# Transposes of nine pre-norm tile passes: TensorE against the DMA crossbar

## The chip, the cores and the metric

The kernel runs on the eight cores of one Trainium2 chip. Every core runs the same program on its own share: half of one stream (2,048 frames in four tiles of 512) and two of the sixteen running streams (32 rows). Nothing is exchanged between cores. The metric is the time of the slowest core, in microseconds of device time. A core has a matrix engine (TensorE, PE), a vector engine (VectorE, DVE), a scalar engine (ScalarE, ACT), a general engine (GpSimd, POOL) and a sync engine (SyncE, SP). Each works through its own list of instructions in order and waits on semaphores; SP and POOL issue the DMAs.

## The reference

One layer has three sub-layers, each of which reads its input through a norm ("pre-norm") and adds a normed result to it:

```
def rmsnorm(x, g):
    y = x32 * lax.rsqrt(jnp.mean(jnp.square(x32), axis=-1, keepdims=True) + EPS)
    return (y * g).astype(x.dtype)

# sub-layer 1: pooling and a gated convolution of width 3 on xn @ w_in, group norms
xn = rmsnorm(x, g_mix_pre)
...
x = x + rmsnorm(merged @ w_out, g_mix_post)
# sub-layer 2: attention into 256 memory tokens, 4 heads of 256
x = x + rmsnorm(cross_attn(rmsnorm(x, g_x_pre), mem_k, mem_v, w_q, w_co), g_x_post)
# sub-layer 3: MLP 1024 -> 4096 -> 1024
hid = jnp.square(jax.nn.relu(rmsnorm(x, g_ff_pre) @ w_up))
x = x + rmsnorm(hid @ w_down, g_ff_post)
```

The pre-norm has two factors: one per row (the reciprocal root of the mean square) and one per column (g).

## The kernel before

The stream's rows lie on the 128 partitions when they are loaded (X, 128 rows x 1024 columns, fp32, eight buffers). A matmul needs the 1024 columns on the partitions. So each sub-layer begins, for each of the four tiles, with a **tile pass** (`pre_tile`, line 800): for each of four row tiles of 128 it calls `pre_sub` (line 759). That squares X on ScalarE with a sum (the output of the square, which nobody reads, goes into the buffer xs), makes the row factor of it in two small ScalarE instructions (Ln and Exp), scales X by it on VectorE into xs (bf16), transposes the eight 128x128 blocks of xs on TensorE into one PSUM bank, and brings the bank into xT on VectorE, multiplied by the column factors (gcs). There are two xs buffers and two xT buffers; xT holds one tile, 128 partitions x 8 blocks x 512 rows, bf16. Three sub-layers of four tiles are twelve tile passes; the memory tokens and the 32 rows of the running streams call `pre_sub` by themselves.

The consumers of xT are, per tile, the mixer's projections (`win`, in `pool_group` and `conv_group`), the query projections (`wq`, `qproj`, 64 matmuls) and the up-projection (`up_chunk`, 256 matmuls, weights up in three buffers of 1 MB, each of which POOL refills when TensorE has released it). A tile of attention is: query projections into qT, four heads (scores, the exponential pT on ScalarE, its sum and the value products on TensorE, the reciprocal rd in two ScalarE instructions, the product mg on VectorE), the output projection `wco`, and `post`, which adds to X. The MLP has a down-projection of 256 matmuls (`wdn`) after each up-projection. The order of tiles in attention is 2, 3, 0, 1; the X of tiles 0 and 1 was stored to x1 and is loaded again there.

The program is first written down as a list of operations with what they read and write. A planner (`Prog.schedule`, line 245) then gives each engine its order: at each moment it takes, of the operations that are ready by its own costs, the one written down first (`prio`), if PSUM has banks for it. A DMA is planned with 2.6 us and its bytes at 345 GB/s on SP (lines 242 and 243), 3.4 us for 256 KB. The emitted lists are fixed: on the chip an engine stands at an instruction whose semaphores are late, and all that follows in its list stands with it. Nearly all instructions are recorded by helpers, so one line of the profile stands for many: L633 matmuls, L638 transposes, L662 activations, L669 VectorE's products of two tensors, L677 its products with a column, L682 its three-operand form, L690 and L692 copies, L701 DMAs.

Of the kernel before, what the change touches and what calls it, by code (L numbers as in the profile page):

```python
# [9 lines left out]
AF = mybir.ActivationFunctionType  # L10
ALU = mybir.AluOpType
# [6 lines left out]
TN = 512  # L18
NSUB = 4
# [493 lines left out]
def build_program():  # L513
# [161 lines left out]
    def ts(out, in0, s1, op0, per=0.5):  # L675
        rdl = [in0] + ([] if isinstance(s1, float) else [s1])
        P.add([("dve", lambda e, L: e.tensor_scalar(out=L(out), in0=L(in0), scalar1=s1, scalar2=None, op0=op0),  # L677
                c_dve(ncols(out), per))], reads=rdl, writes=[out])
# [34 lines left out]
    def r3(ap, n):  # L713
        return ap.rearrange("p (c t) -> p c t", c=n)
# [6 lines left out]
    def stat(r, n=1):  # L721
        a = stn[0]
        stn[0] += n
        assert stn[0] <= 512
        return st[0:r, a:a + n]
# [24 lines left out]
    def rstd(ss, r):  # L750
        a = stat(r)
        b = stat(r)
        act(a, ss, AF.Ln, scale=1.0 / D, bias=epsb[0:r, 0:1])
        act(b, a, AF.Exp, scale=-0.5)
        return b
# [3 lines left out]
    def pre_sub(X, r, gc, dst):  # L759

        ss = stat(r)
        xs = xsr[xs_n[0] % 2][0:r, :]
        xs_n[0] += 1
        act(xs, X, AF.Square, accum=ss)
        rs = rstd(ss, r)
        ts(xs, X, rs, ALU.mult)
        ps = PS(1, reserve=1)
        for c in range(8):
            tr(ps.v(0, 128, c * 128, c * 128 + r, BF16), xs[:, c * 128:(c + 1) * 128], idb[0:r, 0:r])
        src = ps.v(0, 128, 0, 1024, BF16, lambda a: r3(a, 8)[:, :, 0:r])  # L770
        gb = gcs[:, gc * 8:(gc + 1) * 8].unsqueeze(2).to_broadcast([128, 8, r])
        tt(dst, src, gb, ALU.mult)
# [17 lines left out]
    def load_tile(t, src, lead=LEAD):  # L790
# [6 lines left out]
            ops.append(load(b[:, :], src[row:row + 128, :], 524288, lead=lead, rd=(src is not xp)))  # L797
        return ops

    def pre_tile(t, gc, buf):  # L800
        for i in range(NSUB):
            dst = r3(buf[:, :], 8)[:, :, i * 128:(i + 1) * 128]
            pre_sub(Xof[(t, i)][:, :], 128, gc, dst)
# [393 lines left out]
    def load_down(a, b, after=None):  # L1197
        for k in range(a, b):
            wload(dparts[k][:, :], wdn_d, 8 * k, 8 * k + 8, after)
# [57 lines left out]
    for t in range(2, NT):  # L1257
        for g in range(4):
            step(pool_group(t, g))
            if t == 2:  # L1260
                kv_block(g)
                if g < 2:
                    kv_loads(g + 2)
        for cc in range(4):
            step(conv_group(t, cc))
            if cc == 1 and t + 1 < NT:
                pre_tile(t + 1, 0, xT[(t + 1) % 2])
            elif cc == 1:
                pre_tile(2, 1, xT[0])
        step(None)  # L1270
        if t == NT - 1:
            state_out()
            wload(wco[:, :], wco_d, 0, 16)
        else:
            wload(wq[:, :], wq_d, 0, 16)
        mix_out(t)
# [3 lines left out]
    for p, t in enumerate((2, 3, 0, 1)):  # L1280
        for j in range(8):
            qproj(p, j)
        if p == 1:
            smp_q()
        if p == 3:
            load_down(2, 4)
        fins = []
        for hh in range(4):
            step(attn_head(p, hh))
            if hh == 1 and p < 3:  # L1290
                pre_tile((3, 0, 1)[p], 1, xT[(p + 1) % 2])
            elif hh == 1:
                pre_sub(Xe[0:NS, :], NS, 2, r3(xTe[:, :], 8)[:, :, 0:NS])
                pre_tile(0, 2, xT[0])
        step(None)
        if p == 1:
            smp_attn()
            load_down(0, 2)
        out_tile(t, lambda kc, p=p: mg[p % 2][:, kc * TN:(kc + 1) * TN], 8, wc, gslot["g_x_post"],
                 x2 if t >= 2 else None)  # L1300
        if p < 2:
            load_tile(p, x1)
        if p == 0:
            for k in range(3):
                load_up(0, k)
        if p == 1:
            out_smp(lambda kc: mgs[:, kc * NS:(kc + 1) * NS], 8, wc, gslot["g_x_post"])
    load_gp("g_ff_post")
    ups = None
    for t in range(NT):  # L1310
        for k in range(8):
            for jj in range(4):
                up_chunk(t, k * 4 + jj)
            if t == 0:
                if k % 4 == 0:
                    ups = PS(1)
                up_smp(k, ups)
            n = k + 3
            if n < 8:
                op = load_up(t, n)  # L1320
                if t == 0 and n == 7:
                    load_down(4, 8, op)
            elif t + 1 < NT:
                load_up(t + 1, n - 8)
        if t + 1 < NT:
            pre_tile(t + 1, 2, xT[(t + 1) % 2])
        out_tile(t, hid, 32, wd, gslot["g_ff_post"], yp)
        if t == 0:
            out_smp(lambda kc: hids[:, kc * NS:(kc + 1) * NS], 32, wd, gslot["g_ff_post"])
            dma("sp", ysm[:, :], Xe[0:NS, :], NS * 4096, wr=False)  # L1330
        if t + 2 < NT:
            load_tile(t + 2, x2)
# [100 lines left out]
```

How the kernel before makes its waits and increments, by code:

```python
        def run(e, eng):  # L458
            seen = {}
            for op in seqs[e]:
                waits = {}
                for p in plan[op]:
                    k, v = (p.sem, p.semval) if p.is_dma else (p.eng, p.sigval)
                    if seen.get(k, 0) >= v:
                        continue
                    if waits.get(k, 0) < v:
                        waits[k] = v
                for k, v in waits.items():
                    eng.wait_ge(dsem[k] if isinstance(k, tuple) else esem[k], v)
                    seen[k] = v
                ins = op.fn(eng, lambda x: x.resolve(psum) if isinstance(x, PV) else x)
                if op.is_dma:
                    ins.then_inc(dsem[op.sem], 16)
                elif op.needs_signal:
                    ins.then_inc(esem[e], 1)
            if e == "sp":
                for k, last in dma_last.items():
                    if seen.get(k, 0) < last.semval:
                        eng.wait_ge(dsem[k], last.semval)
```

The softmax here doesn't subtract the row's maximum and nothing guards it: scores larger than these inputs give would overflow.

## Time and profile before

| | us |
|---|---|
| median of 3 runs (915.09, 916.25, 1033.09) | 916.25 |
| the profiled execution | 913.83 |
| its span, slowest core | 912.3 |
| the eight cores' spans | 901.6 to 912.3 |
| TensorE, busy time in the span | 858.4 |
| VectorE | 396.1 |
| ScalarE | 383.8 |
| GpSimd | 113.4 |

The highest of the three runs fell into a disturbed state of the chip and is left out of comparisons. Engine busy times count the instructions' own durations, overlaps taken out; since matmuls overlap one another (each is listed with some 0.38 us and begins 0.216 us after the one before), distances between starts tell what a matmul costs. In rows of the timeline, a number in brackets at the end is the time for which the engine was idle before, and what ended that. In rows of a stretch ("A:B") the numbers are its length, then the busy times of PE, PEld, DVE, ACT and POOL with their instruction counts, the granted TensorE clock (1.00 is the 2.4 GHz level), the mean busy share of the DMA engines, and GB/s. In rows of DMA issues: how often, KB each, median us from issue to landing.

### The profile page before, as it was taken

How to read it: one execution, taken by the hardware profiler on the slowest of the kernel's cores; microseconds unless marked ns; L12 is line 12 of the kernel's file. 1: busy time of each engine (PE TensorE's matmuls, PEld its weight loads, DVE VectorE, ACT ScalarE, POOL GpSimd, SP SyncE). 2: the span in 40 equal slices, each digit the busy share in tenths (PEclk: the TensorE clock that was granted, in tenths of full speed). 3: DMA queues.
4: the chain of work that ended last, by engine and by line, in shares of the span. 5: the costliest groups of instructions: out<-in, count | busy, mean ns of one | idle time of the engine just before them, and what ended most of it. 6: DMA issues, size and time to landing. Idle time of an engine off the chain costs nothing.

```text
span 912.3 us, 13810 instructions; the slowest of 8 cores (901.6 to 912.3 us)
## 1 busy us (share of the span) xinstructions
PE 858.4 (94%) x4708; PEld 407.1 (45%) x4708; DVE 396.1 (43%) x545; ACT 383.8 (42%) x808; POOL 113.4 (12%) x164
## 2 busy tenths in 40 slices
PE   1679998899999999999999999999999999999996
PEld 1334445444445454445445444444444444444442
DVE  4547659566875556546523131323222412222212
ACT  4456647556776565656434031332223410133101
POOL 4363100611520000000012000110001100010000
PEclk9989999999999999999999999999999999999999
DMA  9994054952459629006499962698218981088011
GB/s 236 146 156 64 1 174 149 199 87 44 63 82 174 192 50 241 13 1 93 73 147 145 155 175 70 95 152 129 73 66 145 142 129 47 32 122 124 1 46 47
DMA packets 69801, 97.61 MB, mean 107 GB/s; under 512 B 2618, under 2 KB 60218, under 8 KB 69732
## 3 DMA queue, kind: packets, MB, share of 16 engines
q0 software_dynamic: 58384, 58.85, 46.3%
q1 hardware_dynamic: 11348, 37.87, 12.1%
q8 instruction: 39, 0.64, 0.3%
q14 instruction: 30, 0.25, 0.1%
HBM read 137.50 MB, written 18.07 MB: 171 GB/s over the span
## 4 chain that ended last, share of the span: by engine, by line
PE 85%; DMA 8%; DVE 2%; ACT 2%; issue 1%; SPq 0%; POOL 0%; DVEq 0%; ACTq 0%; POOLq 0%
PE ps L633 83%; PE ps L638 2%; DMA wkv_108<-w_v 2%; DMA win<-w_in 1%; DMA up_129<-w_up 1%; DMA X_63<-xp 1%; DMA x<-X_65 1%; DMA O_58<-mem 1%; DMA X_65<-x 1%; DVE O_58 L669 0%; DVE mg_83 L669 0%; ACT rf_106 L662 0%; SPq L701 0%; ACT sq_104 L662 0%; DVE xT_55 L669 0%
## 5 line engine op out<-in xcount | busy, mean ns | idle before, releaser
L669 DVE TENSOR_TENSOR O_57<-ps,gp 128x1024 f32<-128x1024 f32 (+1 forms) x26 | 31.7, 1221 | 120.0 <-PE ps L633 73.7
L662 ACT ACTIVATE O_57<-ps 128x1024 f32<-128x1024 f32 (+1 forms) x26 | 26.5, 1021 | 125.0 <-PE ps L633 123.6
L669 DVE TENSOR_TENSOR O_58<-ps,gp 128x1024 f32<-128x1024 f32 (+1 forms) x25 | 30.6, 1222 | 96.0 <-PE ps L633 61.9
L662 ACT ACTIVATE rt_128<-ps 128x512 bf16<-128x512 f32 x64 | 38.2, 597 | 72.5 <-PE ps L633 64.5
L662 ACT ACTIVATE rt_127<-ps 128x512 bf16<-128x512 f32 x64 | 38.2, 596 | 70.3 <-PE ps L633 70.3
L633 PE MATMUL ps<-xT_55,win 128*128 128x512 bf16 x256 | 62.8, 395 | 4.6 <-DVE xT_55 L669 2.5
L662 ACT ACTIVATE O_58<-ps 128x1024 f32<-128x1024 f32 (+1 forms) x25 | 25.6, 1023 | 96.0 <-PE ps L633 94.6
L633 PE MATMUL ps<-xT_56,win 128*128 128x512 bf16 x256 | 62.2, 394 | 0.4 <-DVE mg_84 L682 0.4
L633 PE MATMUL ps<-xT_56,up_129 128*128 128x512 bf16 x192 | 42.4, 379 | 0.5 <-DMA up_129<-w_up 0.4
L633 PE MATMUL ps<-xT_55,up_130 128*128 128x512 bf16 x192 | 42.4, 379 | 0.0
L633 PEld LDWEIGHTS ps<-xT_55,win 128*128 128x128 bf16 x256 | 25.1, 101 | 34.9 <-issue 9.3
L633 PEld LDWEIGHTS ps<-xT_56,win 128*128 128x128 bf16 x256 | 25.7, 101 | 32.5 <-issue 5.8
L669 DVE TENSOR_TENSOR xT_56<-ps,gcs 128x1024 bf16<-128x1024 bf16 x24 | 28.9, 1219 | 22.5 <-PE ps L638 22.2
L669 DVE TENSOR_TENSOR xT_55<-ps,gcs 128x1024 bf16<-128x1024 bf16 x24 | 28.9, 1218 | 16.2 <-PE ps L638 10.6
L633 PE MATMUL ps<-xT_56,up_131 128*128 128x512 bf16 x160 | 35.4, 379 | 0.0
L633 PE MATMUL ps<-xT_56,up_130 128*128 128x512 bf16 x160 | 35.3, 379 | 0.0
L633 PE MATMUL ps<-xT_55,up_129 128*128 128x512 bf16 x160 | 35.3, 379 | 0.0
L633 PE MATMUL ps<-xT_55,up_131 128*128 128x512 bf16 x160 | 35.3, 379 | 0.0
L633 PE MATMUL ps<-wdn_132,hid_123 128*128 128x512 bf16 x128 | 33.5, 379 | 0.0
L633 PE MATMUL ps<-wdn_135,hid_124 128*128 128x512 bf16 x128 | 33.2, 379 | 0.0
L633 PE MATMUL ps<-wdn_134,hid_124 128*128 128x512 bf16 x128 | 33.0, 379 | 0.0
L633 PE MATMUL ps<-wdn_133,hid_123 128*128 128x512 bf16 x128 | 33.0, 379 | 0.0
(356 smaller groups left out, 1521.4 us busy)
## 6 DMA issues: line engine op xcount, KB each, us to landing
up_129<-w_up POOLq DMA_DIRECT2D x11, 1024.0 KB, 11.4
up_130<-w_up POOLq DMA_DIRECT2D x11, 1024.0 KB, 12.3
up_131<-w_up POOLq DMA_DIRECT2D x10, 1024.0 KB, 10.8
win<-w_in POOLq DMA_DIRECT2D x4, 768.0 KB, 27.7
wout<-w_out POOLq DMA_DIRECT2D x1, 2048.0 KB, 46.2
wq<-w_q POOLq DMA_DIRECT2D x1, 2048.0 KB, 16.5
wco<-w_co POOLq DMA_DIRECT2D x1, 2048.0 KB, 16.3
X_61<-xp SPq DMA_DIRECT2D x2, 512.0 KB, 6.4
```

The costliest lines, as they stand in the source:

```text
L633: P.add([("pe", lambda e, L: e.matmul(L(out), lhsT=lhsT, rhs=rhs, start=start, stop=stop, skip_group_check=True), max(0.03, n * 0.000421 + ...
L638: P.add([("pe", lambda e, L: e.transpose(out=L(out), in_=in_, identity=idn), 0.065 if in_.dtype == BF16 else 0.25)], reads=[in_, idn], wri ...
L662: return e.activation(out=L(out), in_=L(in_), func=func, scale=scale, **kw)
L669: opts.append(("dve", lambda e, L: e.tensor_tensor(out=L(out), in0=L(in0), in1=L(in1), op=op), c_dve(n, per)))
```

## The change

`pre_tile_dma` takes the place of `pre_tile` in nine of the twelve passes: the mixer's tile 3, the four of attention and the four of the MLP. The mixer's first three passes, the memory tokens and the running streams keep `pre_sub`. In the new function xs is transposed by one DMA per row tile (`dma_start_transpose`, from SBUF into SBUF, 256 KB, on SP's queue), which writes straight into xT. The column factor is then applied in place, after all four row tiles have landed, by eight VectorE instructions of 128x512, one for each block of columns. The planner is told 0.06 us for the issue, 262,144 bytes, and a quarter of the usual cost per element for the eight products.

In attention the pass for the next tile is also written down earlier: ahead of the four heads, not after the second one. So it stands before all of them in `prio`.

```
+    def pre_tile_dma(t, gc, buf):
+        for i in range(NSUB):
+            X = Xof[(t, i)][:, :]
+            ss = stat(128)
+            xs = xsr[xs_n[0] % 2][:, :]
+            xs_n[0] += 1
+            act(xs, X, AF.Square, accum=ss)
+            rs = rstd(ss, 128)
+            ts(xs, X, rs, ALU.mult)
+            dst = r3(buf[:, :], 8)[:, :, i * 128:(i + 1) * 128]
+            P.add([("sp", lambda e, L, dst=dst, xs=xs: e.dma_start_transpose(out=dst, in_=xs), 0.06)],
+                  reads=[xs], writes=[dst], nbytes=262144)
+        for c in range(8):
+            v = buf[:, c * TN:(c + 1) * TN]
+            ts(v, v, gcs[:, gc * 8 + c:gc * 8 + c + 1], ALU.mult, per=0.25)
...
             if cc == 1 and t + 1 < NT:
-                pre_tile(t + 1, 0, xT[(t + 1) % 2])
+                pre_tile_dma(t + 1, 0, xT[(t + 1) % 2])
             elif cc == 1:
-                pre_tile(2, 1, xT[0])
+                pre_tile_dma(2, 1, xT[0])
...
+        if p < 3:
+            pre_tile_dma((3, 0, 1)[p], 1, xT[(p + 1) % 2])
+        else:
+            pre_sub(Xe[0:NS, :], NS, 2, r3(xTe[:, :], 8)[:, :, 0:NS])
+            pre_tile_dma(0, 2, xT[0])
         fins = []
         for hh in range(4):
             step(attn_head(p, hh))
-            if hh == 1 and p < 3:
-                pre_tile((3, 0, 1)[p], 1, xT[(p + 1) % 2])
-            elif hh == 1:
-                pre_sub(Xe[0:NS, :], NS, 2, r3(xTe[:, :], 8)[:, :, 0:NS])
-                pre_tile(0, 2, xT[0])
...
         if t + 1 < NT:
-            pre_tile(t + 1, 2, xT[(t + 1) % 2])
+            pre_tile_dma(t + 1, 2, xT[(t + 1) % 2])
```

The planner makes a new order of it. Three places, all in the third attention pass (p = 2), in which X_65 to X_68 are the four row tiles of the next pass. First ScalarE, before (a row with xs on the left is a Square, pT the exponential, rd the reciprocal, qT the eviction of a query projection):

```order
L662 ACTIVATE xs_59,st<-X_65 128x1024 [waits d_sp_13]
L690 ACTIVATE qT_112<-ps 128x512 [waits s_pe]
L662 ACTIVATE st<-st,epsb 128x1 [waits s_act]
L662 ACTIVATE st<-st 128x1 [waits s_act]
L662 ACTIVATE xs_60,st<-X_66 128x1024 [waits d_sp_15]
L662 ACTIVATE st<-st,epsb 128x1 [waits s_act]
L662 ACTIVATE st<-st 128x1 [waits s_act]
L690 ACTIVATE qT_112<-ps 128x512 [waits s_pe] x4
L662 ACTIVATE pT_116<-ps 128x1024 [waits s_pe]
L662 ACTIVATE pT_117<-ps 128x1024 [waits s_pe]
L662 ACTIVATE xs_59,st<-X_67 128x1024 [waits d_sp_17,s_dve,s_pe]
```

and now:

```order
L662 ACTIVATE xs_60,st<-X_66 128x1024 [waits d_sp_32,d_sp_26]
L690 ACTIVATE qT_112<-ps 128x512 [waits s_pe]
L662 ACTIVATE st<-st,epsb 128x1 [waits s_act]
L662 ACTIVATE st<-st 128x1 [waits s_act]
L690 ACTIVATE qT_112<-ps 128x512 [waits s_pe]
L662 ACTIVATE xs_59,st<-X_67 128x1024 [waits d_sp_33,s_dve,d_sp_35]
L690 ACTIVATE qT_112<-ps 128x512 [waits s_pe]
L662 ACTIVATE st<-st,epsb 128x1 [waits s_act]
L662 ACTIVATE pT_116<-ps 128x1024 [waits s_pe]
L662 ACTIVATE st<-st 128x1 [waits s_act]
L662 ACTIVATE pT_117<-ps 128x1024 [waits s_pe]
L662 ACTIVATE xs_60,st<-X_68 128x1024 [waits d_sp_34,s_dve,d_sp_36]
```

The third Square (X_67) stood behind both exponentials and waited for TensorE's transposes; it now stands ahead of them, among the query projections, and waits for d_sp_35, the first transposing DMA.

VectorE, before:

```order
L677 TENSOR_SCALAR xs_60<-X_66,st 128x1024 [waits d_sp_15,s_act]
L669 TENSOR_TENSOR xT_56<-ps,gcs 128x8x128 [waits s_pe] x2
L669 TENSOR_TENSOR mg_83<-ps,rd_118 128x512 [waits s_act]
L669 TENSOR_TENSOR mg_83<-ps,rd_118 128x512
L677 TENSOR_SCALAR xs_59<-X_67,st 128x1024 [waits d_sp_17,s_act]
L677 TENSOR_SCALAR xs_60<-X_68,st 128x1024 [waits d_sp_18,s_act]
L669 TENSOR_TENSOR xT_56<-ps,gcs 128x8x128 [waits s_pe] x2
L669 TENSOR_TENSOR mg_83<-ps,rd_119 128x512 [waits s_act]
```

and now:

```order
L677 TENSOR_SCALAR xs_59<-X_67,st 128x1024 [waits d_sp_33,s_act]
L669 TENSOR_TENSOR mg_83<-ps,rd_118 128x512 [waits s_pe,s_act]
L677 TENSOR_SCALAR xs_60<-X_68,st 128x1024 [waits d_sp_34,s_act]
L669 TENSOR_TENSOR mg_83<-ps,rd_118 128x512 [waits s_pe]
L669 TENSOR_TENSOR mg_83<-ps,rd_119 128x512 [waits s_pe,s_act]
L677 TENSOR_SCALAR xT_56<-xT_56,gcs 128x512 [waits d_sp_35,d_sp_36,d_sp_37,d_sp_38]
L677 TENSOR_SCALAR xT_56<-xT_56,gcs 128x512 x7
L669 TENSOR_TENSOR mg_83<-ps,rd_119 128x512 [waits s_pe]
```

The four evictions out of PSUM are gone; eight products wait for all four DMAs and have five of the eight mg products of the pass behind them.

TensorE there, now (idle spots aside, no transposes are left between the heads):

```order
L633 MATMUL ps<-pT_117,vS 128x512 [waits s_dve]
L633 MATMUL ps<-pT_117,vS 128x512
L633 MATMUL ps<-pT_116,ones 128x512 [waits s_act]
L633 MATMUL ps<-pT_116,ones 128x512
L633 MATMUL ps<-pT_116,vS 128x512 x2
L633 MATMUL ps<-pT_116,vS 128x512 [waits s_dve]
L633 MATMUL ps<-pT_116,vS 128x512
L633 MATMUL ps<-pT_117,ones 128x512 [waits s_act]
L633 MATMUL ps<-pT_117,ones 128x512
L633 MATMUL ps<-pT_117,vS 128x512 x4
L633 MATMUL ps<-wco,mg_83 128x512 [waits s_dve]
```

Between its waits for VectorE it has six, then eight matmuls.

## Rows read from the trace of the kernel before

**Rows 1.** The page: engines' busy time, and the chain that ended last, by line.

```profile
PE 858.4 (94%) x4708; PEld 407.1 (45%) x4708; DVE 396.1 (43%) x545; ACT 383.8 (42%) x808; POOL 113.4 (12%) x164
...
PE ps L633 83%; PE ps L638 2%; DMA wkv_108<-w_v 2%; DMA win<-w_in 1%; DMA up_129<-w_up 1%; DMA X_63<-xp 1%; DMA x<-X_65 1%; DMA O_58<-mem 1%; DMA X_65<-x 1%; DVE O_58 L669 0%; DVE mg_83 L669 0%; ACT rf_106 L662 0%; SPq L701 0%; ACT sq_104 L662 0%; DVE xT_55 L669 0%
```

**Rows 2.** Stretches of the span: loads and first tiles, mixer and attention, MLP.

```profile
0.00:190.00 190.00, 151.05 (x892) 75.27 (x892) 113.40 (x175) 106.25 (x233) 58.34 (x98) 0.96 0.68 138
190.00:426.00 236.00, 230.01 (x1399) 111.06 (x1398) 153.75 (x175) 149.68 (x314) 26.14 (x33) 1.00 0.52 98
426.00:903.90 477.90, 477.30 (x2422) 220.73 (x2420) 126.47 (x194) 126.25 (x258) 28.95 (x33) 1.00 0.59 100
```

**Rows 3.** Groups by form: count, busy us, mean ns, idle before.

```profile
L638 PE MATMUL ps<-idb,xs_60 128*128 128x128 bf16 x200 | 17.2, 226 | 7.3 <-DVE xs_60 L677 7.2
```

**Rows 4.** Timeline of TensorE at the end of an up-projection: start, us.

```profile
624.72 0.61 PE L638 MATMUL ps<-idb,xs_59 128*128 128x128 bf16 x8
625.17 0.81 PE L633 MATMUL ps<-wdn_132,hid_123 128*128 128x512 bf16 x3
```

**Rows 5.** Groups by form, VectorE: eviction into xT, scaling into xs, the square.

```profile
L669 DVE TENSOR_TENSOR xT_56<-ps,gcs 128x1024 bf16<-128x1024 bf16 x24 | 28.9, 1219 | 22.5 <-PE ps L638 22.2
L669 DVE TENSOR_TENSOR hid_123<-rt_127 128x512 bf16<-128x512 bf16 x16 | 6.8, 425 | 16.2 <-ACT rt_127 L662 16.2
L677 DVE TENSOR_SCALAR xs_60<-X_67,st 128x1024 bf16<-128x1024 f32 x4 | 3.0, 748 | 0.8 <-ACT st L662 0.8
```

**Rows 6.** DMA issues of 256 KB on SP.

```profile
mk<-O_58 SPq DMA_DIRECT2D x1, 256.0 KB, 4.0
mk<-O_57 SPq DMA_DIRECT2D x1, 256.0 KB, 8.5
mv<-O_58 SPq DMA_DIRECT2D x1, 256.0 KB, 3.2
mv<-O_57 SPq DMA_DIRECT2D x1, 256.0 KB, 2.3
```

**Rows 7.** The page: busy tenths of the DMA engines in 40 slices of 22.8 us.

```profile
DMA  9994054952459629006499962698218981088011
```

**Rows 8.** The MLP: issues and landing of up blocks, their use, TensorE's wait.

```profile
583.87 0.87 POOL L701 DMA_DIRECT2D up_129<-w_up  x1 [7.49 <-PE ps L633]
688.05 0.87 POOL L701 DMA_DIRECT2D up_130<-w_up  x1 [59.86 <-PE ps L633]
...
595.54 7.07 PE L633 MATMUL ps<-xT_56,up_129 128*128 128x512 bf16 x32
...
up_129<-w_up POOLq DMA_DIRECT2D x11, 1024.0 KB, 11.4
...
L633 PE MATMUL ps<-xT_56,up_129 128*128 128x512 bf16 x192 | 42.4, 379 | 0.5 <-DMA up_129<-w_up 0.4
```

**Rows 9.** Timeline of the third attention pass: two Squares, the last load of X.

```profile
359.01 1.06 ACT L662 ACTIVATE xs_59<-X_65 128x1024 bf16<-128x1024 f32 x1 [1.74 <-DMA X_65<-x]
...
370.85 1.06 ACT L662 ACTIVATE xs_59<-X_67 128x1024 bf16<-128x1024 f32 x1
...
362.82 0.32 SPq L701 DMA_DIRECT2D X_68<-x  x1
```

**Rows 10.** Timeline of VectorE there: the last two evictions, the products behind them.

```profile
376.63 2.36 DVE L669 TENSOR_TENSOR xT_56<-ps,gcs 128x1024 bf16<-128x1024 bf16 x2 [0.71 <-PE ps L638]
378.90 1.28 DVE L669 TENSOR_TENSOR mg_83<-ps,rd_119 128x512 bf16<-128x512 f32 x2
```

**Rows 11.** TensorE there, and the stretch of the heads.

```profile
374.15 1.02 PE L633 MATMUL ps<-qT_112,kT 128*128 128x512 bf16 x4 [0.88 <-DVE mg_83 L669]
375.70 0.38 PE L633 MATMUL ps<-qT_112,kT 128*128 128x512 bf16 x1 [0.53 <-ACT rd_119 L662]
...
368.00:382.00 14.00, 12.35 (x81) 6.13 (x78) 9.57 (x12) 11.91 (x23) 0.00 (x0) 1.00 0.00 0
```

## The prediction

> **What bounds the kernel now.** I read the engines' busy time first. TensorE is busy 94% of the span, no other engine over 45%, and the chain of work that ended last is 83% matmuls of one line and 2% transposes [rows 1]. Then I cut the span into stretches [rows 2]. Up to 190 us TensorE also waits for loads (151 of 190 us busy). From 190 to 426 us (last mixer tiles, attention) it is idle 6.0 us, from 426 us to its end (the MLP) 0.6 us. The granted clock there is 1.00. So in 714 us of the 912 us there is next to nothing to win but TensorE's own work, and work taken off it shows almost one for one, unless a new wait appears. All nine passes that the change touches put their transposes into this part; a few of the first pass fall just before it.
>
> **Step 1, what is removed.** There are 400 full-size bf16 transposes, 200 out of each of the two xs buffers [rows 3]: 12 tile passes and the two memory tiles, 50 row tiles of 8. Nine passes are 36 row tiles, 288 transposes. Their own duration, 226 ns, overlaps the next one's, so I take the distance between starts: a run of eight begins at 624.72, the next matmul at 625.17 [rows 4], 0.45 us per row tile. 36 × 0.45 = **16.2 us** of TensorE. With them go 36 evictions of 1.22 us on VectorE [rows 5], 4.9 us a pass, and a PSUM bank for each.
>
> **Step 2, what is added: 36 crossbar DMAs of 256 KB on SP's queue.** No row shows one. Call T the time from issue to landing. The nearest rows are the other 256 KB transfers that SP issues, both between SBUF and HBM: 2.3, 3.2, 4.0 and 8.5 us [rows 6]; the two longer ones belong to the eighth slice of the span, where the DMA engines are at 9 tenths, the two shorter to the ninth, at 5 [rows 7]. I take 3.5 us, among the three lower ones, because of the slices from 274 to 433 us, in which the attention passes lie, the DMA share is 9 in two, 6 in two and 2 or less in three; 2.3 and 8.5 are the bounds. Against this speaks the Trainium skill, "VectorE: DVE Perf Modes", the section on the three transpose paths, which gives 1309 ns for a 128x128 bf16 block through the crossbar and 390 ns on TensorE. Eight blocks one after another would make an estimate of T of 10.5 us, and the sum below would then come out slower than before. No run here shows either figure.
>
> Where T falls decides. In the three MLP passes the result is wanted a whole down-projection later (in one of them POOL stood 59.86 us for TensorE [rows 8]), so I cost them at nothing; cover gone, it is rival A. In the six others three engines wait in order. ScalarE's third Square writes the buffer that the first DMA still reads, and the order shows it in front of the exponentials. In the third attention pass the first and third Squares were 11.84 us apart (359.01 and 370.85) [rows 9], so T under some 8 us hides there; the new order moves them closer, which is free while TensorE does projections. VectorE waits longer: the eight column products wait for all four DMAs and stand ahead of the attention products (the mg rows), for which TensorE waits. The row that ends the last scaling now has two products (0.64 us each, 1.28 for two [rows 10]) before that wait, so VectorE stands T − 1.3 us.
>
> **Step 3, the column products.** A 128x512 product of bf16 in SBUF by a column has no row. The scaling of 1024 columns from fp32 takes 0.75 us, half of that 0.37; the bf16 square of two inputs 0.425 [rows 5]. I take 0.37, 3.0 us a pass. In the same place VectorE was idle 0.71 us and evicted for 2.36 [rows 10], 3.1 us. So a pass makes VectorE later by (T − 1.3) + 3.0 − 3.1 = T − 1.4, at T = 3.5 by 2.1 us, six times 12.6 us. That is the upper end, if TensorE pays all of it. The lower end is a gain: the Squares leave the crowded head phase, VectorE does less, and the 6.6 us of idle time in the two stretches could go. Of +12.6 and −6.6 I take the middle, **+3 us**: ScalarE was a cause of TensorE's waits in those passes (0.53 us for a reciprocal, 0.88 us for a product [rows 11]), which helps, and the wait for the DMA is new, which does not.
>
> SP's own queue: it issues the stores and loads of X as before, and issuing takes some 0.3 us each. In the third attention pass its four DMAs stand behind the last load of X, which was issued at 362.82 [rows 9], 3.8 us after the first Square began; a row tile takes nearly that long to be scaled, so it costs about a microsecond, and that lies before the wait above. POOL's loads are not passed by anything. The clock is at its 2.4 GHz level throughout (1.00), so there is nothing to gain or lose in it.
>
> **Sum.** 913.83 (the profiled execution, span 912.3 and 1.5 around it) − 16.2 + 3 = 900.6. The median of the three runs is 916.25 and the lowest 915.09, 2.4 and 1.3 above that execution; I add 1.9: **902.5 us**. Its own range is 892.9 (16.2 and 6.6 gained) to 912.1 (16.2 gained, 12.6 lost).
>
> **Rivals.**
> A, the weight stream. In the MLP a 1 MB block of up weights is issued when a buffer is released and lands in 11.4 us; one issued at 583.87 was used at 595.54, 11.7 us later [rows 8], so little is spare. Four transposes move as much as one block through the same 16 DMA engines. At 2.3 us each that is 9.2 us; if a third of it meets the loads (four of a tile's twelve block times), that is some 3 us a tile, 9 us in three: 911.5. For it: the DMA share there is near full [rows 7] and TensorE waited for such a load already [rows 8]. Against it: the new order has two of the three tiles loaded, and so transposed, mostly in the down-projection before, in which POOL issues nothing (up to 688 us in the row). Chance 0.12.
> B, slower: the crossbar DMA is long. If T is 8.5, VectorE is late by T − 1.4 = 7.1 us in each of six passes. TensorE has some 2 us of work there that needs no product of VectorE's (six and eight matmuls between its waits for VectorE in the new order, of 7.07/32 = 0.22 us each [rows 8], 3.0 in all, less the waits for ScalarE among them), so it pays 5.1, six times 30.6: 913.8 − 16.2 + 30.6 + 1.9 = 930. It decides from T = 6.1 on, where six times (T − 3.4) eats the 16.2 us. For it: the row of 8.5 us [rows 6], and that the crossbar's cost is in no row; against it: three of the four 256 KB rows are at or under 4 us. Chance 0.15. By the estimate from the page above, T = 10.5, it would be 942.
> C, TensorE's transposes only filled waits. In a head phase, from 368 to 382 us, ScalarE is busy nearly all the time, and TensorE, transposes included, still waited [rows 11]. If ScalarE sets the end there, four attention passes give back nothing: 4 × 4 × 0.45 = 7.2 us less gained, 909.7. Against it: TensorE waited only 6.0 us in 236 [rows 2], and the Squares leave that phase. Chance 0.16.
>
> **Numbers.** My forecast has 0.57. Within 2% of 916.25 means 897.9 to 934.6, about what a measurement of this kernel can tell from no change. Under 897.9 lies the lowest quarter of the forecast's range, 0.14 of the chance; I take 0.13, since A and C can come on top of it. Over 934.6 lies half of B, 0.08. The rest, 0.79, is within. The range 893 to 922 takes in the forecast's own, A and C, and A and C with some of the 12.6; it leaves out most of B and a little below, together under 0.2.
>
> **What would show it.** Step 1: the 128x128 bf16 transposes fall from 400 to 112, and TensorE's busy time by about 16 us. Step 2: the rows of xT from xs on SP land in 3 to 4 us; VectorE's waits for them total under 6 × 2.2 us. Step 3: the new products take 0.2 to 0.4 us each. TensorE's idle time after 190 us should be near 10 us: 25 or more there means B (VectorE waiting for xT's DMAs, TensorE for mg) or A (TensorE waiting for up loads); the same end with 7 us more idle time and no DMA named is C. The forecast is wrong if a DMA lands in over 6 us, or if the stretch before 190 us, which the new order also touches, moves by more than 5 us.

## The result, and the profile after

The changed kernel takes 977.06 us (median of 4 runs, 973.89 to 978.45) beside 916.01 us before: **ratio 1.0665, 95% interval 1.063 to 1.070**, slower by 61 us where 902.5 was forecast. Of the experiments below, replan and all9fix have no ratio, since in all or half of their runs part of the cores ran at a lower granted clock than the rest; their times and spans stand instead.

The profiled execution took 978.45 us, its slowest core (core 6) 976.9. The page's busy times and chain, against [rows 1]:

```profile
PE 865.5 (89%) x4420; PEld 395.5 (40%) x4420; DVE 373.3 (38%) x579; ACT 382.1 (39%) x811; POOL 113.9 (12%) x163
...
PE ps L633 73%; DMA xT_56<-xs_59 3%; DMA xT_55<-xs_59 3%; DMA xT_56<-xs_60 2%; DMA X_67<-xp 2%; DMA up_129<-w_up 1%; DMA win<-w_in 1%; DMA X_63<-xp 1%; PE ps L638 1%; DMA O_57<-mem 1%; SPq L811 1%; DVE xs_59 L677 1%; ACT st L662 1%; DVE xT_
```

The stretches, against [rows 2] (length, busy times of PE, PEld, DVE, ACT, POOL, granted clock, DMA share, GB/s):

```profile
0.00:190.00 190.00, 148.57 (x869) 73.44 (x870) 112.08 (x174) 105.98 (x235) 58.70 (x98) 0.96 0.71 142
190.00:426.00 236.00, 206.17 (x986) 89.47 (x985) 120.50 (x169) 127.78 (x269) 24.36 (x30) 0.90 0.58 108
426.00:976.90 550.90, 510.78 (x2568) 232.64 (x2566) 140.67 (x238) 148.31 (x308) 30.84 (x35) 0.97 0.60 99
```

TensorE was to lose 16.2 us of work; its busy time *rose* by 7.1 us (858.4 to 865.5), and its idle time from 53.9 to 111.4. So the account is: −16.2 for the transposes, +57.5 of idle time, and a remainder of +23.3, beside which stands a lower clock (0.90 and 0.97, where [rows 2] has 1.00): 64.6, the difference of the spans. Worked out from the granted clock during TensorE's busy time, the loss by the clock is 6.4 us before and 30.5 now, 24.1 more. Some 8.5 of it lie in three stretches of 15 us (from 281.7, 340.8 and 380.2 on), in which TensorE was busy throughout and the clock was 0.81; cores 2 and 3, with spans of 964.2 and 961.8 us, have no such stretch, and what brings it is not shown. One of the three:

```profile
340.80:355.80 15.00, 15.00 (x59) 6.20 (x57) 4.48 (x6) 9.34 (x21) 0.00 (x0) 0.81 0.77 203
```

The groups by form show that the change did what it says (against [rows 3, 5]; the products are new):

```profile
L669 DVE TENSOR_TENSOR xT_55<-ps,gcs 128x1024 bf16<-128x1024 bf16 x8 | 9.6, 1217 | 6.0 <-PE ps L633 5.1 <-PE ps L638 1.0
...
L677 DVE TENSOR_SCALAR xT_56<-xT_56,gcs 128x512 bf16<-128x512 bf16 x40 | 11.5, 352 | 24.8 <-DMA xT_56<-xs_59 22.1 <-DMA xT_56<-xs_60 2.7
...
L638 PE MATMUL ps<-idb,xs_60 128*128 128x128 bf16 x56 | 5.1, 244 | 6.7 <-DVE xs_60 L677 6.7
```

112 transposes are left of 400, 12 evictions of 48, and 72 products cost 0.35 us each. What is out of line is the transposing DMA (L811), by source line: issues on SP, who waited for it, and its time to landing.

```profile
L811 SPq DMA_TRANSPOSE xT_56<-xs_60 x10: 1233/1446/7582, 160.5 to 746.2; - x10
L811 SPq DMA_TRANSPOSE xT_56<-xs_59 x10: 1232/1254/10129, 170.1 to 758.2; - x10
...
  DVE xT_56 L677: 24.8, 3
  ACT xs_59 L662: 19.1, 3
  DVE xT_55 L677: 12.4, 3
  ACT xs_60 L662: 6.2, 2
...
DMA to landing us min/median/max: 3.0/3.1/19.1
```

The median is 3.1 us, the longest 19.1. One by one, 27 of the 36 land in 3.0 to 4.7 us, nine in 10.5 to 19.1. These nine have one thing in common, a load that POOL had issued:

| issued at | landed after, us | loads of POOL in flight then (issue to landing) |
|---|---|---|
| 160.5, 170.1 | 17.5, 16.4 | w_v (157.8 to 173.9, 165.2 to 185.6) |
| 242.0 | 13.8 | wco (239.0 to 257.8) |
| 287.1, 289.1 | 13.7, 19.1 | two of w_up (274.3 to 301.8), ckT, cv (281.4 to 308.9, 282.3 to 314.2) |
| 449.8 | 14.7 | two of w_down (445.6 to 465.3) |
| 499.4, 501.1 | 13.4, 18.6 | three of w_up (495.0 to 520.7) |
| 758.2 | 10.5 | three of w_up (748.1 to 774.1) |

A load that had only just been issued, or was nearly through, cost a DMA under 2 us. Counted in the trace, 1,428 to 2,747 packets of POOL's queue were moved between the issue and the landing of each of the nine; for 24 of the 27 others it was none, for three 8, 253 and 530.

The first attention pass, 284 to 324 us, shows what that cost. Its first two DMAs, from the DMA view of 286:292, and POOL's loads of that time:

```profile
xT_56<-xs_59 SPq DMA_TRANSPOSE x1, 13.7
xT_56<-xs_60 SPq DMA_TRANSPOSE x1, 19.1
```

```profile
281.44 0.88 POOL L701 DMA_DIRECT2D kTs<-ckT  x1 [5.38 <-PE ps L633]
282.31 0.89 POOL L701 DMA_DIRECT2D vSs<-cv  x1
```

ScalarE there; in brackets the idle time before and what ended it:

```profile
300.95 1.06 ACT L662 ACTIVATE xs_59<-X_67 128x1024 bf16<-128x1024 f32 x1 [6.54 <-DMA xT_56<-xs_59]
302.00 1.00 ACT L662 ACTIVATE pT_116<-ps 128x1024 bf16<-128x1024 f32 x1
...
308.34 1.06 ACT L662 ACTIVATE xs_60<-X_68 128x1024 bf16<-128x1024 f32 x1 [5.15 <-DMA xT_56<-xs_60]
...
309.78 1.00 ACT L662 ACTIVATE pT_117<-ps 128x1024 bf16<-128x1024 f32 x1
```

The third and fourth Square (X_67, X_68) write the xs buffers that these DMAs still read, and an exponential (pT) stands right behind each. VectorE, and then TensorE:

```profile
286.87 0.75 DVE L677 TENSOR_SCALAR xs_60<-X_66,st 128x1024 bf16<-128x1024 f32 x1
309.68 0.75 DVE L677 TENSOR_SCALAR xs_59<-X_67,st 128x1024 bf16<-128x1024 f32 x1 [22.07 <-ACT st L662]
...
316.21 2.19 DVE L677 TENSOR_SCALAR xT_56<-xT_56,gcs 128x512 bf16<-128x512 bf16 x8 [2.74 <-DMA xT_56<-xs_60]
318.32 1.28 DVE L669 TENSOR_TENSOR mg_83<-ps,rd_119 128x512 bf16<-128x512 f32 x2
```

```profile
303.15 1.01 PE L633 MATMUL ps<-pT_116,ones 128*128 128x512 bf16 x2 [6.08 <-ACT pT_116 L662]
...
310.93 1.01 PE L633 MATMUL ps<-pT_116,vS 128*128 128x512 bf16 x2 [4.77 <-ACT st L662]
...
321.95 3.49 PE L633 MATMUL ps<-wco,mg_83 128*128 128x512 bf16 x10 [2.21 <-DVE mg_83 L669]
```

VectorE stood 22.07 us for the row factor of the third row tile, then waited for the last DMA with mg behind the products; TensorE waited for the exponential (6.08), for the next one (4.77; it went on 0.15 us after that one's end) and for mg (2.21). It then ran slowly as well. The same stretch of the span, now and before:

```profile
284.00:324.00 40.00, 26.92 (x149) 11.19 (x148) 10.85 (x21) 16.13 (x31) 0.00 (x0) 0.76 0.94 146
```

```profile
284.00:324.00 40.00, 39.13 (x254) 19.03 (x252) 23.79 (x26) 23.87 (x51) 0.00 (x0) 1.00 0.78 173
```

Here, with 13.1 us of idle time in it, the clock is 0.76 on average over 40 us; before it was 1.00.

In the fourth attention pass the DMA issued at 449.8 held ScalarE's fourth Square for 11.04 us, with the reciprocals behind it, and so TensorE:

```profile
468.58 6.71 PE L633 MATMUL ps<-wco,mg_84 128*128 128x512 bf16 x20 [11.67 <-DVE mg_84 L669]
```

In the MLP, VectorE and TensorE at the end of the first up-projection:

```profile
503.68 0.43 DVE L669 TENSOR_TENSOR hid_124<-rt_128 128x512 bf16<-128x512 bf16 x1 [0.85 <-ACT rt_128 L662]
519.84 0.62 DVE L677 TENSOR_SCALAR xT_56<-xT_56,gcs 128x512 bf16<-128x512 bf16 x2 [15.74 <-DMA xT_56<-xs_59]
520.37 0.42 DVE L669 TENSOR_TENSOR hid_124<-rt_127 128x512 bf16<-128x512 bf16 x1
```

```profile
520.94 0.58 PE L633 MATMUL ps<-wdn_134,hid_124 128*128 128x512 bf16 x1 [12.62 <-DVE hid_124 L669]
```

The planner had put the second tile's pass into the up-projection; its products stand ahead of hid, which the down-projection reads.

Where the time goes stage by stage (us from the span's start, worked out as the median of the eight cores; a few matmuls that stand ahead of the long run of their stage are left out):

| first matmul of | before | after | stage up to it: longer by | long DMAs in it |
|---|---|---|---|---|
| query projections | 265.1 | 278.4 | 13.3 | 3 |
| wco, pass 1 | 292.2 | 320.6 | 15.1 | 2 |
| wco, pass 2 | 332.9 | 365.0 | 3.7 | 0 |
| wco, pass 3 | 377.1 | 414.4 | 5.2 | 0 |
| wco, pass 4 | 418.2 | 466.0 | 10.5 | 1 |
| wdn, tile 1 | 492.2 | 558.1 | 18.1 | 2 |
| wdn, tile 2 | 619.6 | 681.1 | −4.4 | 0 |
| wdn, tile 3 | 731.9 | 797.1 | 3.7 | 1 |
| wdn, tile 4 | 844.5 | 906.3 | −3.4 | 0 |
| (end of wdn) | 897.7 | 959.6 | 0.1 | 0 |

The five stages with a long DMA lost 61 us, the five without lost 1.

### The profile page after: what moved, and what is told of

Its sections match the earlier page's. It is cut to its first block, busy times and chain, and to the rows that moved or that the text cites. A ratio compares the mean times of both kernels' runs of the same rounds, so it can differ in the third digit from the quotient of the medians.

```text
span 976.9 us, 13473 instructions; the slowest of 8 cores (961.8 to 976.9 us)
## 1 busy us (share of the span) xinstructions
PE 865.5 (89%) x4420; PEld 395.5 (40%) x4420; DVE 373.3 (38%) x579; ACT 382.1 (39%) x811; POOL 113.9 (12%) x163
## 3 DMA queue, kind: packets, MB, share of 16 engines
q1 hardware_dynamic: 49364, 47.31, 18.1%
## 4 chain that ended last, share of the span: by engine, by line
PE 74%; DMA 14%; DVE 4%; ACT 3%; issue 3%; SPq 1%; POOL 0%; ACTq 0%; DVEq 0%; POOLq 0%
PE ps L633 73%; DMA xT_56<-xs_59 3%; DMA xT_55<-xs_59 3%; DMA xT_56<-xs_60 2%; DMA X_67<-xp 2%; DMA up_129<-w_up 1%; DMA win<-w_in 1%; DMA X_63<-xp 1%; PE ps L638 1%; DMA O_57<-mem 1%; SPq L811 1%; DVE xs_59 L677 1%; ACT st L662 1%; DVE xT_56 L677 0%; ACT xs_59 L662 0%
## 5 line engine op out<-in xcount | busy, mean ns | idle before, releaser
L633 PE MATMUL ps<-xT_55,up_130 128*128 128x512 bf16 x192 | 44.0, 387 | 4.2 <-ACT rt_128 L662 2.9
L633 PE MATMUL ps<-wdn_134,hid_124 128*128 128x512 bf16 x128 | 33.7, 381 | 12.6 <-DVE hid_124 L669 12.6
L633 PE MATMUL ps<-xT_56,up_129 128*128 128x512 bf16 x192 | 42.4, 379 | 1.9 <-DMA up_129<-w_up 1.9
L633 PE MATMUL ps<-wco,mg_84 128*128 128x512 bf16 x128 | 32.2, 418 | 12.8 <-DVE mg_84 L669 11.7
L633 PE MATMUL ps<-xT_55,up_129 128*128 128x512 bf16 x160 | 36.8, 390 | 0.0
L633 PE MATMUL ps<-xT_56,up_131 128*128 128x512 bf16 x160 | 35.4, 379 | 0.0
L633 PE MATMUL ps<-xT_55,up_131 128*128 128x512 bf16 x160 | 35.3, 379 | 0.0
L633 PE MATMUL ps<-xT_56,up_130 128*128 128x512 bf16 x160 | 35.3, 379 | 0.0
L633 PE MATMUL ps<-wco,mg_83 128*128 128x512 bf16 x128 | 29.9, 394 | 5.1 <-DVE mg_83 L669 5.1
L633 PE MATMUL ps<-wdn_132,hid_123 128*128 128x512 bf16 x128 | 33.5, 379 | 0.0
L633 PE MATMUL ps<-wdn_133,hid_123 128*128 128x512 bf16 x128 | 33.3, 379 | 0.0
L633 PE MATMUL ps<-wdn_135,hid_124 128*128 128x512 bf16 x128 | 33.2, 379 | 0.0
## 6 DMA issues: line engine op xcount, KB each, us to landing
up_129<-w_up POOLq DMA_DIRECT2D x11, 1024.0 KB, 11.6
up_130<-w_up POOLq DMA_DIRECT2D x11, 1024.0 KB, 13.2
wq<-w_q POOLq DMA_DIRECT2D x1, 2048.0 KB, 18.1
wco<-w_co POOLq DMA_DIRECT2D x1, 2048.0 KB, 18.8
```

The costliest lines, as they stand in the source:

```text
L633: P.add([("pe", lambda e, L: e.matmul(L(out), lhsT=lhsT, rhs=rhs, start=start, stop=stop, skip_group_check=True), max(0.03, n * 0.000421 + ...
```

## The experiments

**Theory**: a transposing DMA moves 256 KB as 1,024 packets of 256 B, and these take turns with the packets of a weight load on the same DMA engines; where the two meet it is long, and the in-order engines pass the wait on. **Rivals**: the crossbar itself is slow in company; the new order, the buffers or the wait as such cost, whatever the DMA takes. In the diffs, − is the changed kernel unless said otherwise. Ratios are to the kernel before on the same chip, with 95% intervals. Only copy256 has the changed kernel's order on TensorE, VectorE and ScalarE, instruction for instruction; after every other edit the planner made another order, so those times hold its effect too, and the landings of the DMAs are the firmer evidence.

**1. mlp3 and six: which passes.** mlp3 has `pre_tile_dma` in the MLP's three passes alone, with the order of before in attention; six has it in the other six alone (`pre_tile(t + 1, 2, ...)` in the MLP).

> Only the three passes of the MLP go by DMA; the other nine are as in the kernel before. Turn-taking theory (a transposing DMA is 1,024 packets of 256 B and each waits for the packets of a weight load that is in flight on the same DMA engines; without one it lands in 3.1 us): one or two of the twelve DMAs fall into an up load and take 10 us or more, and cover hides most of it: 916 - 5.4 (12 row tiles of 0.45 us) + 0 to 5 = 911 to 916. Rival A of the prediction (the DMAs delay the up loads): 919 or more, with TensorE waiting for up blocks by 9 us more than before.

> Only the mixer's tile 3 and the four passes of attention (and the first of the MLP, written there) go by DMA; the three MLP passes keep TensorE. Turn-taking theory: eight of the nine long DMAs of the changed kernel (13 to 19 us) lie here, so nearly the whole loss is here: 970 to 980. If the loss were spread evenly over the nine passes: 916 + 61 x 6/9 = 957.

Measured: mlp3 1.0027 (0.9994 to 1.0061), six 1.0526 (1.0500 to 1.0553). Most of the loss is in the six, but at 958.8 us less than the 970 to 980 expected and close to the 957 of an even spread. The expectation had miscounted: six of the nine long DMAs lie in these passes, not eight (and six has six, of 14.1 to 20.0 us). The two parts, 0.3 and 5.3%, make less than the 6.7% of all nine together. In mlp3 two of twelve DMAs were long (8.3 and 10.2 us); the second, a last row tile beside an up load, made VectorE wait with hid behind it, then ScalarE, and so TensorE:

```profile
704.46 3.57 PE L633 MATMUL ps<-xT,up 128*128 128x512 bf16 x8 [4.02 <-ACT rt L662]
```

With a clock of 0.50 (the 1.2 GHz level) in 703.7:710.3, that takes back the 5.4 us gained. Rival A's price did not show: of TensorE's waits over 0.5 us one was for an up load, 2.3 us.

**2. copy2k and copy256: the crossbar, or the packets?**

```
- e.dma_start_transpose(out=dst, in_=xs)
+ e.dma_start(out=dst, in_=xs)           # copy2k, with dst = buf[:, i * D:(i + 1) * D]
+ e.dma_start(out=dst, in_=r3(xs, 8))    # copy256, dst as it was
```

> Each transposing DMA is replaced by a plain copy of the same 256 KB in rows of 2 KB (128 packets, no transposition; xT holds wrong values). Everything else as in the changed kernel, order included. Turn-taking theory: 8 packets for each DMA engine wait at most some 200 ns each beside a weight load, so all 36 land in 2.5 to 5 us, and the time is what the prediction's sum gives for such a T: 900 to 914. If the wait on the DMA or the new order as such is the loss, whatever T: over 940. If the crossbar is the slow part: also 900 to 914, so copy256 has to tell it from turn-taking.

> Each transposing DMA is replaced by a plain copy of the same 256 KB into pieces of 256 B (1,024 packets, no transposition; xT holds wrong values). Turn-taking theory: 3 us alone and 10 to 19 us beside a weight load, as the transposing one, 965 to 985. If the crossbar (transposing as such) is what is slow in company: under 6 us everywhere, and 900 to 914.

Measured: copy2k **1.0031** (1.0016 to 1.0046), copy256 **1.0669** (1.0629 to 1.0708), the changed kernel's own ratio without a transposition. copy256 has nine landings of 13.2 to 21.5 us, the others 2.8 to 4.8. The first two DMAs of the first attention pass in copy256, and the four of that pass in copy2k:

```profile
xT<-xs SPq DMA_DIRECT2D x2, 256.0 KB, 17.9
```

```profile
xT<-xs SPq DMA_DIRECT2D x4, 256.0 KB, 7.5
```

The crossbar is out: the same order with plain copies in 256 B pieces loses as much. The size of the pieces counts. But copy2k's landings missed their expectation of 2.5 to 5 us: eleven of its DMAs still took 6.5 to 9.4 us beside a load (2.2 to 4.7 else). Company costs a transfer of few packets too. Its time, 913.6 us, is at the upper end of the expected 900 to 914 and that of before; but against its expectation the order changed with the destination in xT, so the time is not the price of the pieces alone.

**3. replan, junk, xs3, noprod: who passes the wait on?**

```
replan:  - reads=[xs], writes=[dst], nbytes=262144)
         + reads=[xs], writes=[dst], nbytes=2310000)
junk:    - act(xs, X, AF.Square, accum=ss)
         + act(xj[:, :], X, AF.Square, accum=ss)     # a scratch buffer, in pre_tile_dma
xs3:     - xsr = [fix("xs%d" % i, D, BF16) for i in range(2)]
         + xsr = [fix("xs%d" % i, D, BF16) for i in range(3)]   # and % 3 where it is used
noprod:  - for c in range(8): ... ts(v, v, gcs[...], ALU.mult, per=0.25)
```

> The changed kernel, but the planner is told 2.31 MB for a transposing DMA in place of 262,144 bytes, that is 9.3 us alone and 16 us beside a weight load in its model; what is transferred is unchanged. If the loss is an order made for 3.4 us, in which ScalarE and VectorE stand at late DMAs with other work behind them: most of it goes, 900 to 930. If the passes have no other work to put there (two xs buffers, the result needed soon), so that no order hides 14 to 19 us: over 945. I lean to the middle, 935, since the wait of ScalarE for xs stays whatever the order.

> In the changed kernel the Square's output, which nobody reads, goes to a scratch buffer of its own in the nine passes, so ScalarE never waits for a transposing DMA (in the changed kernel it did for 25 us in five waits, with exponentials behind it); VectorE's scaling still does. If ScalarE's waits are what TensorE pays: about 25 us of waits and half of the clock loss behind them gone, 940 or less against 977. If the wait only passes on to VectorE's scaling and its products (mg behind them): 965 to 980.

> A third xs buffer in the changed kernel: the third row tile of a pass waits for no DMA, the fourth for the first one. If the two-buffer ring is the limit: about the gain of the scratch buffer for the Square, 935 to 955. If the products' wait for all four DMAs is the limit: 965 to 980.

> The changed kernel without the 72 column products (the column factor is left out of nine passes), so VectorE does not wait for the DMAs of a finished tile; TensorE does, where it reads xT. In the changed kernel VectorE waited 37 us for xT in six waits. If that wait, with mg products behind it, is what TensorE pays: 930 or less. If the wait for xs ahead of it is: 960 to 975, since the last DMA is issued as late as before.

Measured: junk 1.0287 (1.0253 to 1.0322), xs3 1.0223 (1.0201 to 1.0245), noprod 1.0329 (1.0283 to 1.0375). junk came as its first expectation has it; xs3, at 931.3 us, just under its first; noprod, at 941.6, between its two. Each of the three alone takes back half of the loss or more, while DMAs beside loads still take up to 18 to 20 us. replan took 947.4 to 948.8 us in six runs, the kernel before 909.7 to 912.4; in each of them two or four cores had spans of 940 to 947 us, the others 917 to 934. What the planner's wrong price was worth stays open; its new order put sixteen DMAs beside loads (7.3 to 22.4 us), not nine. So the long DMA is the cause, and how much of it TensorE pays is a matter of who stands behind it: ScalarE with the exponentials, VectorE with mg or hid. In junk the wait partly moved to VectorE's scaling (who waited for the DMAs, us and times):

```profile
  DVE xT L678: 24.9, 6
  DVE xs L678: 18.8, 2
  ACT xs L663: 0.5, 1
```

The sizes are not clean prices, by the changed orders. For xs3, experiment 5 shows a third buffer to be worth 10 us without any DMA.

**4. earlype, all9fix, mlp9, best17: the move alone, both fixes, and only short DMAs.** earlype keeps the move in attention and all transposes on TensorE. all9fix has three xs buffers and the Square writing to `dst`. The other two:

```
mlp9:    - pre_tile_dma(t + 1, 2, xT[(t + 1) % 2])
         + pre_tile_dma(t + 1, 2, xT[(t + 1) % 2], 3)   # row tiles 0 to 2; pre_sub for the fourth
         and pre_tile, in its old place, in all other passes
best17:  mlp9, three xs buffers, and
         + if p in (1, 2): pre_tile_dma((3, 0, 1)[p], 1, xT[(p + 1) % 2])   # ahead of the heads
```

> No transposing DMA at all; only the move is kept: in attention the next tile's pass, with TensorE's transposes, is written ahead of the heads. If the loss is the DMA's time beside weight loads and the move only its setting: within 5 us of the kernel before (906 to 917 against some 911). If the move itself is at fault (Squares and scalings ahead of exponentials and mg): 925 or more.

> All nine passes by DMA as in the changed kernel, with three xs buffers, and the Square's unread output goes to the place in xT that the DMA fills afterwards, so ScalarE waits for no DMA and VectorE's scaling only in a pass's fourth row tile. If the two fixes take away the same wait (they gave 42 and 37 us alone): 925 to 932, as with three buffers alone. If they add: 905 to 920. Either way the DMAs beside weight loads still take 13 us or more.

> Three MLP passes by DMA for row tiles 0 to 2, TensorE for the fourth row tile, which alone came late and met an up load (10.2 us, TensorE stood 4.0 us and its clock fell behind it). All else as before. Nine row tiles of 0.45 us less on TensorE and no long DMA in its way: 4 us less than before, ratio 0.994 to 0.998. If the DMAs cost the up loads as much: 1.000 or more.

> The MLP as in mlp9, the second and third attention passes by DMA (no weight load was in flight in them; all eight landed in 3.0 to 3.8 us), three xs buffers, the other passes on TensorE as before. 17 row tiles of 0.45 us are 7.7 us: 903 to 906 against some 911, ratio 0.991 to 0.996. If a short DMA already costs its gain in VectorE's order in attention (the sum's T - 1.4 a pass): 0.996 to 1.000.

Measured: earlype 0.9986 (0.9969 to 1.0004), so the move costs nothing by itself. all9fix took 928.8 and 935.5 us in the two runs that can be compared, against 912.1, with DMAs of up to 18.8 us: the fixes do not add. mlp9 0.9946 (0.9927 to 0.9965), as expected; best17 0.9890 (0.9868 to 0.9912), somewhat better than its 0.991 to 0.996, and for a wrong reason: its trace was 10.7 us ahead at the first query projection, before any transposing DMA.

**5. bef3, mlp9x3: what is the third buffer, what the crossbar?** bef3 is the kernel before with `range(3)` for xs; mlp9x3 is mlp9 with it.

> The kernel before, all transposes on TensorE, with a third xs buffer and nothing else. best17 was 10 us faster than before, yet in its trace TensorE reached attention 10.7 us earlier, ahead of its first transposing DMA. If the third buffer alone does that: ratio 0.987 to 0.992, and best17 owes nothing to the crossbar. If it is the DMAs (by another order in the mixer): 0.998 to 1.002.

> Three xs buffers, and of the MLP's three passes row tiles 0 to 2 by DMA; attention on TensorE. Nine row tiles are 4 us: if the third buffer gives 10 and they add, 898 against 912, ratio 0.984 to 0.988, the fastest so far. If the third buffer gives nothing of its own: 0.994 to 0.996, as mlp9.

Measured: bef3 **0.9894** (0.9871 to 0.9916), mlp9x3 **0.9835** (0.9811 to 0.9859), 897.52 us against 911.87, just under the 898 expected and the fastest kernel with the whole computation. The third buffer alone gives best17's gain; nine row tiles by DMA in the MLP give 0.6% more, some 5 us (4 forecast). So best17's eight row tiles in attention, all short, *lost* 4.6 us against mlp9x3. By the stage medians its second pass took 42.2 us (40.4 in mlp9x3) and its third 49.4 (44.8).

**6. streamdma and streampe: company, put where there was none.** best17 and mlp9x3, each with

```
+ if p == 1 and i == 1:      # hook of out_tile: after the second row tile of the output
+     for k in range(3):
+         wload(up_slot[(0, k)][:, :], wup_d, 8 * k, 8 * k + 8, last)
```

> best17 with company put beside the four DMAs of the third attention pass, which landed in 3.1 to 3.8 us there: three 1 MB blocks of up weights are loaded a second time, with the same values into the same buffers, from the end of the pass before on. If a weight load in flight makes a transposing DMA long: these four take 8 to 19 us, and the time is 8 to 25 us over best17, 910 to 927. If what made the nine of the changed kernel long was something else of their places (X loads, stores on their own queue): under 5 us, and within 3 us of best17.

> Control for streamdma: the same second loads of the three blocks in mlp9x3, whose attention has no transposing DMA. They meet the X loads alone: within 4 us of mlp9x3. If the loads themselves cost as much as in streamdma: 10 us or more above mlp9x3, and streamdma says nothing of the DMAs.

The four DMAs of the third pass in best17, then the first and the second of them in streamdma:

```profile
xT<-xs SPq DMA_TRANSPOSE x4, 3.4
```

```profile
xT<-xs SPq DMA_TRANSPOSE x1, 14.0
```

```profile
xT<-xs SPq DMA_TRANSPOSE x1, 13.7
```

The third took 7.3 us, the fourth, after the loads had landed, 3.1. Company made the DMAs long in a place where they had been short. The price is less clean: streamdma 1.0079 (1.0053 to 1.0106) is 17.6 us over best17, but the control missed its 4 us: 0.9937 (0.9914 to 0.9960), 9.1 us over mlp9x3, close to the 10 from which on it was to say nothing of the DMAs. In its trace the two X loads of that pass with a landing on record took 9.4 and 9.6 us, 5.4 and 4.2 in mlp9x3. Some 8 us remain as an estimate for the DMAs.

**7. np17: why short DMAs lose in attention.** best17 with `for c in range(8 if gc == 2 else 0)`: no column products in its two attention passes.

> best17 without the 16 column products of its two attention passes (the column factor is left out there). In best17 those two passes took 1.8 and 4.5 us more than in mlp9x3, with DMAs of 3 to 4 us and 1.8 us less of TensorE each. If VectorE's products, which wait for all four DMAs and have mg behind them, cost that: 6 us and more come back, 893 to 897. If it is the Squares and scalings placed ahead of the heads, or the last load of X: 900 to 903, as best17.

Measured: 0.9834 (0.9798 to 0.9871), 895.81 us, 6.3 less than best17 and as expected: it is the products, with the order that they bring. VectorE in best17's third pass, and TensorE after it:

```profile
365.10 0.67 DVE L669 TENSOR_TENSOR mg<-ps,rd 128x512 bf16<-128x512 f32 x1
365.83 2.19 DVE L677 TENSOR_SCALAR xT<-xT,gcs 128x512 bf16<-128x512 bf16 x8
367.94 0.68 DVE L669 TENSOR_TENSOR mg<-ps,rd 128x512 bf16<-128x512 f32 x1
```

```profile
368.77 0.59 PE L633 MATMUL ps<-pT,vS 128*128 128x512 bf16 x2 [1.40 <-DVE mg L669]
```

One mg, then 2.19 us of products, then the next mg, for which TensorE stood 1.40 us and ScalarE, with its next reciprocal, 2.92.

## Why the prediction was wrong, step by step

**What bounds the kernel: right.** TensorE is the bound from 190 us on, and work taken off it shows if no wait comes in its place (mlp9, mlp9x3).

**Step 1: right.** 288 transposes went, and nine row tiles brought 4.9 us (mlp9) and some 5 (mlp9x3 against bef3) where 0.45 us each make 4.

**Step 2 is the step that failed**: "I take 3.5 us ...; 2.3 and 8.5 are the bounds." The value was good for 27 DMAs and no bound for the other nine. It failed in the reading of the view, in two ways. A DMA share of a 22.8 us slice says nothing of the moment at which a DMA is issued; the question was which load POOL has in flight then, and the timeline of POOL would have told it for every pass. The row of 8.5 us was itself such a meeting: it was issued at 167.13, after w_v loads of 159.36 and 166.74 that took 20.8 and 20.0 us to land, and 744 packets of POOL's queue were moved in its time; in those of the 4.0, 3.2 and 2.3 us it was 0, 96 and 0. And the 256 KB transfers of [rows 6] resemble the new one in bytes, not in packets. What decides is shown by the packets of 292:300 in the changed kernel (queue, packets, MB, share): POOL's loads against the transposing DMA, and in 402:410 two transposing DMAs alone.

```profile
q0 software_dynamic: 1106, 1.11, 90.3%
q1 hardware_dynamic: 1070, 0.27, 30.3%
```

```profile
q1 hardware_dynamic: 2112, 0.52, 35.0%
```

1,106 packets against 1,070: one for one, though one's are four times as large. At 134 a microsecond, 1,024 packets take 7.7 us, after some 4 us from issue to the first (14 packets under 512 B in 287.2 to 291.4): most of the 13.7. That turns are taken packet by packet is inferred from these equal counts; why the first comes so late (4.0 to 6.6 us after the issue in the six long DMAs that stood behind no other transposition, 1.2 alone) is open. The Trainium skill, "DMA: Bandwidth & Descriptors", section "Queues, rings and completion order", says that an engine goes in turn round the queues that have work, one packet of typically some 9 to 17 descriptors at a time. The equal counts agree with such turns, but do not show how many of the profile's packets make one. The other page of the Trainium skill, "VectorE: DVE Perf Modes", by which the prediction weighed 942, pointed to the right side by a wrong road: alone, eight blocks land in 3.1 us, 0.38 us a block and not 1.3.

Three statements fell with T. "Free while TensorE does projections" (the Squares): ScalarE stood 6.54 and 5.15 us for the DMAs, with exponentials behind. "So I cost them at nothing" (the MLP): the second tile's pass stands in the up-projection, not in the down-projection, and cost 12.62 us of idle time; the fourth tile's last DMA met an up load. And SP's queue was put at "about a microsecond": three times a second DMA behind a first took 7.4 to 10.1 us to issue beside loads, 1.2 alone, and the load of X_67 behind the first long one landed 18.2 us after its issue.

**The clock**: "nothing to gain or lose in it" read a row that had no long waits in it. Idle spells of 6.08, 11.67 and 12.62 us came with 0.76 to 0.77 in the stretches around them (284:324, 445:475, 495:525). With smaller ones and the three stretches at 0.81, the lower clock makes the remainder of 23.3 us in the account.

**Step 3**: the products cost what was taken (0.35 against 0.37 us, 2.19 for eight in a run). Their place was under-priced: T − 1.4 and the 1.8 us gained leave +0.3 us a pass; best17 measured +1.8 and +4.6, since each mg behind the products holds TensorE and then ScalarE.

**Rivals.** A: hardly seen; it was the loads that delayed the DMAs (by buffer, blocks of up took 11.6 to 13.2 us at the median, 10.8 to 12.3 before, and TensorE waited 3.1 us for them, 0.4 before). B had the right sign and half the mechanism: VectorE with mg behind late products. Its 930 at T = 8.5 left out ScalarE, the MLP and the clock, and gave every pass the same T. C: not tested by itself; np17, without the products, took 40.0 and 43.8 us in the two passes (40.4 and 44.8 in mlp9x3), some 1.4 less where 3.6 us of transposes are gone, so a part of C may hold.

## What to carry to other kernels

Before a DMA in small packets is put on a tight path, ask what else is in flight at that very moment, and count packets, not bytes: a mean DMA share hides both. When a buffer's release moves from an engine to a DMA, look at which in-order engine writes that buffer next (here a Square whose output nobody reads) and what stands behind it. And when a version wins, run the part that is not the idea by itself: here a third buffer, without any DMA, was most of the gain.

## What the runs showed of the hardware

- With no packet of a weight load beside it, a 256 KB transposition from SBUF to SBUF lands in 3.1 us at the median (3.0 to 3.8), a copy in 256 B pieces in 3.0 (2.8 to 4.3), in 2 KB rows in 2.3 (2.2 to 4.7). The long ones beside a load take 10.5 to 19.1, 13.2 to 21.5 and 6.5 to 9.4.
- The issue of a transposing DMA takes 1.2 us of SP's queue, a load or store 0.3 to 0.5, a plain copy in 256 B pieces 0.6, and the transposing one up to 10.1 us when the one before it is not through.
- Why a transfer of 128 packets (copy2k) still takes 4 to 7 us longer in company is open; part of it is a late start, as with the transposition.
